# Conditional row sums of a transformer block: where four of them are summed, and by which engines

## The reference, cut to what matters

```python
mod = jax.nn.silu(c) @ w_ada[l] + b_ada[l]            # c: [1, 1024], w_ada: [1024, 6 * 1024]
shift1, scale1, gate1, shift2, scale2, gate2 = jnp.split(mod, 6, axis=-1)
...
mla_out = mla_attention(q_nope, q_pe, k_nope, k_pe, v_mla)      # 4 heads, 1024 positions
d_out = diff_attention(dq[..., 0, :], dq[..., 1, :], dk[..., 0, :], dk[..., 1, :], dv, lam)
...
mix = jnp.concatenate([mla_out, d_out], axis=-1) @ w_out[l]
x = x + gate1[:, None, :] * mix
h2 = rms_norm(x, norm2_g[l]) * (1.0 + scale2[:, None, :]) + shift2[:, None, :]
```

## Time and profile before

| what | value |
|---|---|
| median of 3 runs | 2595.19 us (2594.18 to 2595.61) |
| the profiled execution | 2594.44 us |
| its span, first to last instruction | 2592.8 us |
| mean granted TensorE clock | 0.955 |
| busy over the span | PE 92%, weight loads 74%, DVE 67%, ACT 47%, POOL 19% |
| differential attention with what precedes it | 0 to 457 us |
| latent attention | 457 to 682 us |

### The profile page before, as it was taken

How to read it: one execution, slowest core, us unless ns; L and a number is a source line. 1 busy time by engine, 2 the same in 40 slices (tenths; PEclk the granted TensorE clock), 3 DMA queues, 4 the chain that set the end, 5 groups by cost and what they waited for, 6 DMA issues and landing times. The chain is left out here.

```text
span 2592.8 us, 31607 instructions
## 1 busy us (share of the span) xinstructions
PE 2377.0 (92%) x10766; PEld 1908.7 (74%) x10766; DVE 1729.1 (67%) x1998; ACT 1228.0 (47%) x1643; POOL 491.1 (19%) x474
## 2 busy tenths in 40 slices
PE   5979987898897699999999679999999999999998
PEld 4767765677676588777877558887878888888886
DVE  6378886566585799999999666445357666653344
ACT  5237665556522477767676461111653333332322
POOL 0760000777000010000000200000013332311100
PEclk8989997899897799999999879999999999999999
DMA  6241121339364899999999844433323222244453
GB/s 247 73 142 43 47 68 37 106 91 350 108 200 164 295 398 399 398 399 398 399 398 399 324 168 138 118 118 125 103 66 89 87 83 73 93 155 153 150 174 111
DMA packets 266601, 485.31 MB, mean 187 GB/s; under 512 B 20161, under 2 KB 126094, under 8 KB 265998
## 3 DMA queue, kind: packets, MB, share of 16 engines
q1 hardware_dynamic: 232734, 364.37, 40.4%
q0 software_dynamic: 27440, 98.62, 11.3%
q10 hardware_dynamic: 6336, 21.11, 2.0%
HBM read 402.25 MB, written 76.55 MB: 185 GB/s over the span
## 5 line engine op out<-in xcount | busy, mean ns | idle before, releaser
L2195 DVE TENSOR_TENSOR e_w<-e_raw,e_w 128x1024 fp32r<-128x1024 f32 x384 | 442.3, 1219 | 45.1 <-ACT e_w L2259 44.7
L2259 ACT ACTIVATE e_w<-e_raw 128x1024 fp32r<-128x1024 f32 x384 | 376.5, 1050 | 174.7 <-PE e_pgu L112 143.6
L112 PE MATMUL e_pgu<-e_w,e_xt 128*128 128x512 f32 x1536 | 369.1, 397 | 10.6 <-DVE e_w L2195 5.3
L112 PEld LDWEIGHTS e_pgu<-e_w,e_xt 128*128 128x128 f32 x1536 | 286.1, 189 | 85.2 <-DVE e_w L2195 17.8
L112 PE MATMUL s_ps<-h,s_w 128*128 128x512 f32 x1152 | 268.3, 394 | 2.1 <-DVE h L2623 2.1
L112 PEld LDWEIGHTS s_ps<-h,s_w 128*128 128x128 f32 x1152 | 218.0, 190 | 48.5 <-DVE h L2623 2.3
L112 PE MATMUL w_ps<-w_out,w_ring 128*128 128x512 f32 x1056 | 245.5, 392 | 1.9 <-DVE w_ring L3275 1.9
L112 PE MATMUL w_ps<-y 128*128 128x512 f32 x1056 | 240.2, 389 | 1.4 <-DVE w_o_full L3440 1.0
L112 PEld LDWEIGHTS w_ps<-w_out,w_ring 128*128 128x128 f32 x1056 | 199.3, 189 | 45.0 <-DVE w_out L3282 2.3
L112 PEld LDWEIGHTS w_ps<-y 128*128 128x128 f32 x1056 | 198.0, 188 | 43.4 <-issue 1.4
L112 PE MATMUL w_ps<-y,w_ring 128*128 128x512 f32 x816 | 195.8, 398 | 3.3 <-ACT w_h L3071 3.0
(11 more groups left out here) (437 smaller groups left out, 3967.6 us busy)
## 6 DMA issues: line engine op xcount, KB each, us to landing
e_raw<-in_w_expert_gate_dram SPq DMA_DIRECT2D x128, 512.0 KB, 11.4
e_raw<-in_w_expert_up_dram SPq DMA_DIRECT2D x128, 512.0 KB, 10.5
e_raw<-in_w_expert_down_dram SPq DMA_DIRECT2D x128, 512.0 KB, 10.9
w_raw<-in_ffn_w_gate_up_dram SPq DMA_DIRECT2D x48, 512.0 KB, 6.2
w_o_full<-in_ffn_w_down_dram SPq DMA_DIRECT2D x44, 512.0 KB, 4.0
y_rows<-am_zrow SPq DMA_DIRECT2D x4, 4352.0 KB, 34.3
y_rows<-e_yo ACTq DMA_DIRECT2D x32, 512.0 KB, 6.3
section_rows<-in_ada_w_dram POOLq DMA_DIRECT2D x32, 512.0 KB, 3.9
```

What stands on the lines that cost most here:

```text
L112: o = pe.matmul(out, stat[i], mov[j], start=start and n == 0, stop=stop and n == 2)
L2195: dve.tensor_tensor(w[1][:, slot % CUT], raw[:, slot], w[0][:, slot % CUT].bitcast(F32), ALU.subtract).then_inc(low, 1)
L2259: act.activation(w[0][:, slot % CUT], raw[:, slot], ACT.Copy).then_inc(high, 1)
```

## The change

In the differential attention POOL no longer sums anything: the 36 pieces in quarters, their two buffers and their accumulator are gone. The latent attention now gets all four sections. There, ScalarE scales the rows: after `exponent(s)` it scales one row, 32 rows for 32 steps. POOL loads, adds (7 rows and the bias of each section) and stores. The first scaled row of a section is written by ScalarE straight into the accumulator, so it is ScalarE that now waits for the store of the section before.

```diff
-                diff_attention(nc, g, a, h_t, h_at, first_sections[3:])
+                diff_attention(nc, g, a, h_t, h_at)
...
-            mla_attention(nc, g, a, finished, first_sections[0:3])
+            mla_attention(nc, g, a, finished, first_sections)
```

In `mla_attention`, POOL's loop:

```diff
-                    cond, row = jobs[i][2], rows[t % 2]
-                    pool.wait_ge(part_in[t % 2], 16 * (t // 2 + 1))
-                    if t:
-                        pool.wait_ge(step, t)
-                    if k == 0:
-                        if i:
-                            pool.wait_ge(acc_out, 16 * i)
-                        pool.tensor_scalar(acc[:], row, cond[:, 0:1], None, ALU.mult).then_inc(step, 1)
-                    elif k < KD:
-                        pool.tensor_scalar(row, row, cond[:, k:k + 1], None, ALU.mult).then_inc(part_scaled, 1)
-                        pool.wait_ge(part_scaled, (KD - 1) * i + k)
-                        pool.tensor_tensor(acc[:], acc[:], row, ALU.add).then_inc(step, 1)
+                    row = rows[t % 2]
+                    if k < KD:
+                        pool.wait_ge(part_scaled, KD * i + k + 1)
                     else:
-                        pool.tensor_tensor(acc[0:1, :], acc[0:1, :], row[0:1, :], ALU.add).then_inc(step, 1)
-                    pool.wait_ge(step, t + 1)
+                        pool.wait_ge(part_in[t % 2], 16 * (t // 2 + 1))
+                    if k:
+                        pool.wait_ge(step, KD * i + k - 1)
+                        some = slice(0, P if k < KD else 1)
+                        pool.tensor_tensor(acc[some, :], acc[some, :], row[some, :], ALU.add).then_inc(step, 1)
+                        pool.wait_ge(step, KD * i + k)
                     if t + 2 < pieces:
                         load_piece(pool, jobs[(t + 2) // PIECE], (t + 2) % PIECE, row, part_in[t % 2])
```

and ScalarE's:

```diff
+                def scale_row(u):
+                    i, k = u // KD, u % KD
+                    t = PIECE * i + k
+                    act.wait_ge(part_in[t % 2], 16 * (t // 2 + 1))
+                    if k == 0 and i:
+                        act.wait_ge(acc_out, 16 * i)
+                    act.activation(rows[t % 2] if k else acc[:], rows[t % 2], ACT.Copy, scale=jobs[i][2][:, k:k + 1]).then_inc(part_scaled, 1)
...
                     if s < STEPS:
                         exponent(s)
+                    if s < KD * len(jobs):
+                        scale_row(s)
```

More of the change, by code:

```diff
@@ L126, in rope_rotate, with diff_attention @@
     return dve.tensor_tensor(out, tmp[0:rows, 0, :], tmp[0:rows, 1, :], ALU.add)
-def diff_attention(nc, g, a, h_t, h_at, jobs):
+def diff_attention(nc, g, a, h_t, h_at):
     scale = float(DQK) ** -0.5
@@ L143, in diff_attention @@
                  "maxed nmax expd summed weighted combined probs turned pt_high pt_low vturned v_high v_low pv taken o_out "
-                 "lproj kproj lat_raw squared ssq rooted recip normed lat_high lat_low lat_out kpe_angle kpe_sum kpe_high kpe_low "
-                 "part_in0 part_in1 part_scaled step acc_out")
+                 "lproj kproj lat_raw squared ssq rooted recip normed lat_high lat_low lat_out kpe_angle kpe_sum kpe_high kpe_low")
         (w_in0, w_in1, w_high, w_low, w_used, proj, pj_out, swapped, cos_done, sin_done, roped, qk_high, qk_ready, scored0, scored1,
@@ L148, in diff_attention @@
          o_out, lproj, kproj, lat_raw, squared, ssq, rooted, recip, normed, lat_high, lat_low, lat_out, kpe_angle, kpe_sum, kpe_high,
-         kpe_low, part_in0, part_in1, part_scaled, step, acc_out) = sems(nc, g, " ".join("ad_" + s for s in names.split()))
-        w_in, part_in = (w_in0, w_in1), (part_in0, part_in1)
+         kpe_low) = sems(nc, g, " ".join("ad_" + s for s in names.split()))
+        w_in = (w_in0, w_in1)
         names = ("ident_in c_in lam_in rows_in rows_clear cs_in lat_w_in x_in0 x_in1 x_in2 x_in3 x_in4 x_in5 x_in6 x_in7 "
@@ L187, in diff_attention @@
         r2 = sb("r2", [P, 2])
-        narrow_rows = sb("narrow_rows", [P, 2, QUARTER])
-        narrow = sb("narrow", [P, QUARTER])
-        pieces = PIECE * len(jobs) * (D // QUARTER)
         ps = ctx.enter_context(nc.psum_tensor("ad_ps", [P, 2, T], F32))
@@ L254, in _ @@
             def _(pool):
[L255 to L274, removed]
-                    pool.wait_ge(part_in[t % 2], 16 * (t // 2 + 1))
-                    if t:
-                        pool.wait_ge(step, t)
-                    if k == 0:
-                        if u:
-                            pool.wait_ge(acc_out, 16 * u)
-                        pool.tensor_scalar(narrow[:], row, cond[:, 0:1], None, ALU.mult).then_inc(step, 1)
-                    elif k < KD:
-                        pool.tensor_scalar(row, row, cond[:, k:k + 1], None, ALU.mult).then_inc(part_scaled, 1)
[L284 to L287, removed]
-                    pool.wait_ge(step, t + 1)
[L289 to L293, removed]
                 pool.wait_ge(lat_out, 32)
@@ L1114, in _ @@
                     i, k = t // PIECE, t % PIECE
-                    cond, row = jobs[i][2], rows[t % 2]
[L1116 to L1119, removed]
-                        if i:
-                            pool.wait_ge(acc_out, 16 * i)
-                        pool.tensor_scalar(acc[:], row, cond[:, 0:1], None, ALU.mult).then_inc(step, 1)
-                    elif k < KD:
-                        pool.tensor_scalar(row, row, cond[:, k:k + 1], None, ALU.mult).then_inc(part_scaled, 1)
-                        pool.wait_ge(part_scaled, (KD - 1) * i + k)
-                        pool.tensor_tensor(acc[:], acc[:], row, ALU.add).then_inc(step, 1)
-                    else:
-                        pool.tensor_tensor(acc[0:1, :], acc[0:1, :], row[0:1, :], ALU.add).then_inc(step, 1)
-                    pool.wait_ge(step, t + 1)
+                    row = rows[t % 2]
+                    if k < KD:
+                        pool.wait_ge(part_scaled, KD * i + k + 1)
+                    else:
+                        pool.wait_ge(part_in[t % 2], 16 * (t // 2 + 1))
[4 more added lines that the diff above has]
+                        pool.wait_ge(step, KD * i + k)
                     if t + 2 < pieces:
```

1 line of the change is left out of this document (removed).

## The result

The changed kernel takes 2641.15 us (median of four runs, 2635.55 to 2644.52), the kernel before 2595.09 beside it: a ratio of 1.0174, 95% interval 1.0158 to 1.0190. It is 46 us slower.

What follows compares the result with a forecast made beforehand. The prediction took a loop through ACT, DVE and PE to bound latent-attention steps, PE only around the V product. 14.8 + 33.2 + 8.3 - 2.7 = +53.6 us on 2595.19 gave 2649 us, range 2618 to 2673.

Steps and rivals of the forecast that it cites:

- the likeliest case: Whole kernel: both the step and boundary terms within a third of their size, 2638 to 2662 us, 62 in 100.
- The signs that the prediction named: Changed profile: ACT idle before three scalings, PE idle before three slow V products, exponents 7.7 and 5.8 us apart.
- The steps: Latent attention: each scaling between exponent and copy adds 1.04 us in steps bound by the loop, +14.8 us.
- The boundaries: Latent attention, scalings 8, 16, 24: ScalarE waits for the previous section's store ahead of a needed copy, +33.2 us.
- The clock: V products after the three boundary stalls: PE runs them at a lower clock, 3 x 2.78 = 8.3 us.
- The differential attention: Without POOL's 36 pieces, DVE instructions with two SBUF inputs get shorter there: -2.7 us, bounds 0 and 5.
- GpSimd's last section: End of latent attention: last store and `w_out` rows land before the stage ends, 3 us of cover, cost 0.
- Only the boundaries pay: Rival: PE, not the loop, sets ordinary latent-attention steps; 2634 us, 12 in 100.
- only the steps pay: Rival: stores land early enough or ACT's wait at the boundary is hidden; 2607 us, 7 in 100.
- The clock falls in ordinary steps too: Rival: PE idles more each step, slowing projection and transposes; +18 + 5, 2672 us, 12 in 100.
- Faster: the lock is what matters: Rival: scalings fall into ACT's idle time, and less POOL work frees DVE; -8.4, 2587 us, 4 in 100.
- The Trainium skill's price for the store: Section boundaries: 512 KB store estimated at 3.2 us, each boundary about 3.5 us less, forecast 2638 us.

Runs made afterwards that it cites:

- E10: Not a run: start of the exponent of step 10 in the latent attention; from step 7's exponent to it 17.9 us before, 28.5 changed.
- E18: Not a run: start of the exponent of step 18 in the latent attention; from step 15's exponent to it 18.1 us before, 28.6 changed.
- E26: Not a run: start of the exponent of step 26 in the latent attention; from step 23's exponent to it 17.6 us before, 32.5 changed.
- experiments 5: Changed kernel with a second tile for the sum and each scaling moved from behind the exponent to ahead of the second projection's eviction: 2597.00 us, ratio 1.0018.
- experiment 6: Changed kernel with a second sum tile and bias rows in their own tile: 2609.82 us with scaling behind the exponent, 2588.35 us ahead of the second eviction.
- E0: Not a run: start of the exponent of step 0 in the latent attention; reached after 465.9 us before, 458.0 changed.
- Experiment 4: Changed kernel, one sum; ScalarE scales every row in its slot, GpSimd waits for the store and copies a section's first row into the sum: 2624.80 us.
- the kernel with GpSimd alone: Changed kernel with all four sections in the latent attention, but scaled and added by GpSimd as before: 2606.92 us, ratio 1.0056.
- experiment 1: Changed kernel with a second tile for the sum, so ScalarE's first scaling of a section waits for no store: 2625.97 us, ratio 1.0126.
- loads only: Changed kernel with the 36 narrow loads put back into the differential attention, without arithmetic: 53.8 us from first VectorE instruction to first maximum; no whole time given.
- experiment 7: Second sum tile, bias rows apart, scaling ahead of the second eviction, but the fourth section back on GpSimd in the differential attention: 2590.34 us, ratio 0.9992.
- sums only: Changed kernel with GpSimd's arithmetic put back into the differential attention on zeros, without loads: 55.3 us from first VectorE instruction to first maximum; no whole time given.
- experiment 3: Changed kernel with only three sections in the latent attention, scaled by ScalarE; the fourth stays on GpSimd in the differential attention: 2626.39 us, ratio 1.0127.
- E31: Not a run: start of the exponent of step 31, the latent attention's last; from it to the first `w_out` copy 16.9 us before, 17.9 changed.
- last kernel of experiment 6: Changed kernel with a second sum tile, bias rows in their own tile and scaling ahead of the second eviction: 2588.35 us, ratio 0.9986.

## Why the prediction was right, point by point

- **The whole.** 2649 us against 2641.15, inside the likeliest case. The differences of the terms, in the trace: steps 13.8 for 14.8, boundaries with the clock 35.9 for 41.5, ahead of the stage -7.9 for -2.7, together 41.8 for 53.6 at po. The signs that the prediction named have the right form: ACT idle for the store 7.2, 6.9 and 10.8 us (forecast 8 to 9), TensorE idle 8.4, 8.2 and 12.0 us before the V products (nearly 10), these 5.2 to 6.0 us long (6 to 7), exponents 7.65 and 5.77 us apart (7.7 and 5.8). The median lies 5.6 us above the execution that was traced; that part of the agreement is scatter.
- **The steps.** Right in place and size: E10 to E12 +2.08, E12 to E14 -0.02, E18 to E20 +2.07, E26 to po +5.2 where I had five scalings. The missing 1 us is in head 0, whose first step was 0.7 us shorter. The mechanism is shown by experiments 5 and 6: the cost isn't ScalarE's time, of which the version in the gap spends as much (busy for 158.3 us from E0 to po, 159.4 in the changed kernel), but the copy that was queued behind the scaling. The 13.8 isn't all that the scalings cost: each boundary has two more of them in its chain, which my sum booked there. Without the waits all of them show, 20.2 us (236.9 - 216.7), 1.3 of it the one step at the lower clock.
- **The boundaries.** The arithmetic was right up to the store's issue; the landing was mis-sized. From the issue to the scaling I took 6.79 us from POOL's own waits; measured were 5.33, 5.01 and 8.93. So the new section's scaling starts 14.17 and 13.87 us after the exponent at the first two, not 15.56, and 17.77 at the third, for which I had 17.3. Experiment 4 waits on GpSimd and gets 5.16 for the first, and the kernel with GpSimd alone 6.89, 5.23 and 9.41, so it isn't the waiting engine. Why those behind the load of a weight row differ, 5.0 to 6.9, is open.
- **The clock.** Right that TensorE comes back from the stall at a lower clock, with the size off: the V products take 1.33, 1.72 and 2.07 us longer than 3.90, together 5.1, not 8.3. I took the price from the end of the stage, and that row wasn't the lower bound I called it. That the stall is the cause fits experiment 6, in which it is gone and the products take 3.9 us. But the length of the wait just before them doesn't set the price, as I had assumed ("a longer idle time should do no less"). The kernel of experiment 1 has the same products behind shorter stalls: 5.51 us after 3.01 idle, 3.92 after 3.15, and 6.59, more than any in the changed kernel, after 7.47. What picks one price or the other isn't shown.

```profile
523.55 5.51 PE L1179 MATMUL am_po<-am_pt,am_v 128*128 128x512 f32 x16 [3.01 <-ACT am_pt L1260]
587.35 3.92 PE L1179 MATMUL am_po<-am_pt,am_v 128*128 128x512 f32 x16 [3.15 <-ACT am_pt L1260]
651.99 6.59 PE L1179 MATMUL am_po<-am_pt,am_v 128*128 128x512 f32 x16 [7.47 <-ACT am_pt L1260]
```

- **The boundary as a whole.** At the first two both errors go the same way: I forecast 28.6 us and 2.8 for the clock, 31.4, and measured are 28.5 and 28.6. The V products start 1.4 and 1.7 us sooner than forecast (the landing), and take 1.4 and 1.1 us less (the clock). At the third (32.5 for 32.6) the errors cancel, 0.5 us too little and 0.7 too much; that this one fits so well is luck. And one thing was missing: beneath the store's wait lay a second one, for the section's first row. It changed nothing in the forecast, since the later of the two decides, but it made me promise 2605 us for the second sum.
- **The differential attention.** VectorE's relief was right: 2.9 us by the first `ad_mx`, for 2.7. The stage begins 7.9 us sooner all the same. From that instruction to E0 are 298.3 us before and 293.2 in the changed kernel; in the seven others without GpSimd's arithmetic there (experiments 1, 2, 4, 5, both of 6, loads only) 293.0 to 297.8; in the three others with it 293.5 (experiment 7), 294.7 (sums only) and 298.0 (experiment 3). The two groups overlap, so the further 5 us can't be put down to the change.
- **GpSimd's last section.** Hidden, as forecast: E31 to po is 1.0 us longer, the one scaling.
- **The rivals.** "Only the boundaries pay" falls by the steps, "only the steps pay" by 24.9 us of waiting. "The clock falls in ordinary steps too" shows in single steps of the experiments (8.91 for 7.65 us), and nothing like 12 of them. "Faster: the lock is what matters" had a true mechanism, worth 2.9 us in the differential attention.
- **The Trainium skill's price for the store.** The Trainium skill, "DMA: Bandwidth & Descriptors", section "Anatomy of one DMA — SWDGE (gpsimd) path", gave an estimate of 3.2 us. The landings of the changed kernel, by tile:

```profile
DMA to landing us min/median/max: 3.0/4.9/8.8
```

  Its forecast of 2638 us was nearer than mine, but not by its reason: the 3.0 us is the fourth store, ahead of which POOL had loaded no weight row for a while; the three that are waited for stand 0.6 us behind the load of one (582.30 and 582.87 above) and land in 5.0, 4.9 and 8.8. The kernels with the bias rows apart (experiments 6 and 7) bear on this: they issue a section's store 6 to 7 us behind the last load, and of the six stores between 500 and 600 us five land in 2.9 to 3.0 us, one in 4.1. In the last kernel of experiment 6, from 500 to 600 us:

```profile
DMA to landing us min/median/max: 3.0/3.0/3.0
```

  So in the quiet stretch these traces agree with the estimate of 3.2 us where no load stands just ahead of the store. The third store, with the other traffic, takes 7.2 to 8.5 us even so. No kernel here changes the load ahead and nothing else, so that it is the cause fits, and isn't shown by itself.

## What to carry to other kernels

Before work is put on an engine with idle time, ask what stands behind it in that queue: the same 32 instructions of 1.04 us cost 20 us behind the exponent and nothing ahead of an instruction that waits for another engine anyway. A wait for a DMA belongs in a queue in which nothing urgent follows, and taking it away by a second buffer pays only down to the next thing that is late; look for it (here a row whose slot the bias had taken) before pricing the gain. Take a landing's time from a row with the same transfers just ahead of it and the same traffic beside it: the same 512 KB store landed here in 2.9 to 9.7 us.

## What the runs showed of the hardware that I had not expected

- A 512 KB weight row that GpSimd loads lands, in the last kernel of experiment 6, in 3.7 to 4.2 us between 460 and 500 us, where the core moves 89 GB/s in all, and in 7.0 to 9.3 between 590 and 640, where it moves 376.
- GpSimd copies 128x1024 elements in 1.04 us, where its add takes 2.39 and its scaling 2.85.
- Kernels with the same program up to the latent attention reach E0 at 457.6 to 462.4 us, and TensorE's clock goes with it: from 300 to 457 us its mean is 0.92 in the three that are there by 458.5, 0.89 in the three between 459.1 and 460.5, and 0.88 in the last. The same V product in the changed kernel and in the one with the second sum, on PE:

```profile
371.88 3.91 PE L435 MATMUL ad_po<-ad_pt,ad_v 128*128 128x512 f32 x16
```

```profile
371.19 5.46 PE L435 MATMUL ad_po<-ad_pt,ad_v 128*128 128x512 f32 x16
```

  A gain of that size in an early stage can't be read from one trace.
